# Strassen-Winograd in three more block pairs of one product, with the sum of two branches made by accumulating transfers

## The reference

```python
proj = h @ w_in                 # u, v, q, k, v, gate columns
gate_a, gate_b = jnp.split(jax.nn.sigmoid(gates), 2, axis=-1)
merged = gate_a * (a_out @ w_pa) + gate_b * (b_out @ w_pb)
x = x + merged @ w_o
```

## Time and profile before

| | |
|---|---|
| runs | 1659.09 us median, 1658.59 to 1660.1 |
| profiled execution | 1657.78 us, span 1656.0 us, mean granted clock 0.994 |
| TensorE busy | 1624.0 us (98%) |
| VectorE busy | 1125.3 us (68%) |
| ScalarE busy | 696.1 us (42%) |
| GpSimd busy | 57.6 us (3%) |
| matmuls | 12958, of them 11088 in 462 block products |

### The profile page before, as it was taken

The page is one execution under the profiler, slowest core; times in us unless marked ns, Lnnn a source line. Parts: engine busy times, 40 slices in busy tenths (PEclk is TensorE's granted clock), DMA queues, the critical chain, the costliest instruction groups (busy, mean ns, idle before and its releaser), DMA issues.

```text
span 1656.0 us, 32499 instructions
## 1 busy us (share of the span) xinstructions
PE 1624.0 (98%) x12958; PEld 1584.1 (96%) x12958; DVE 1125.3 (68%) x2053; ACT 696.1 (42%) x1282; POOL 57.6 (3%) x125
## 2 busy tenths in 40 slices
PE   6999999999999999999999999999999999999998
PEld 6999999999999999999999999999999999999997
DVE  6566565656657869652525888888888776767566
ACT  6344444444444426442434544433333334343312
POOL 2000000000000000000012100000000000000001
PEclk8999999999999999999999999999999999999999
DMA  7444434343437774574443233333333327363122
GB/s 246 152 149 117 133 108 135 100 138 101 128 109 206 235 227 154 198 235 132 139 145 107 59 106 105 106 106 106 106 106 104 128 73 267 119 240 104 68 79 109
DMA packets 272473, 227.03 MB, mean 137 GB/s; under 512 B 43336, under 2 KB 223364, under 8 KB 272324
## 3 DMA queue, kind: packets, MB, share of 16 engines
q1 hardware_dynamic: 141054, 158.81, 28.8%
q10 hardware_dynamic: 131269, 66.15, 14.2%
HBM read 150.56 MB, written 74.36 MB: 136 GB/s over the span
## 4 chain that ended last, share of the span: by engine, by line
PE 75%; DVE 2%; DMA 2%; issue 1%; ACT 1%; DVEq 0%; ACTq 0%; POOL 0%; SPq 0%
PE ps L2294 66%; PE ps L2508 3%; DMA lo_f<-g_spill 1%; PE ps L2545 1%; PE ps L2428 1%; PE ps L2370 1%; DMA raw<-in_w_down_dram 1%; PE ps L2400 1%; PE ps L2418 0%; PE ps L2405 0%; PE ps L2388 0%; PE ps L2527 0%; ACT op_hi L1237 0%; DVE w_lo L1605 0%; DVE op_lo L1644 0%
## 5 line engine op out<-in xcount | busy, mean ns | idle before, releaser
L2294 PE MATMUL ps<-op_hi,w_hi 128*128 128x272 f32 x3696 | 780.5, 292 | 14.1 <-issue 5.1
L2294 PE MATMUL ps<-op_hi,w_lo 128*128 128x272 f32 x3696 | 765.9, 289 | 0.0
L2294 PE MATMUL ps<-op_lo,w_hi 128*128 128x272 f32 x3696 | 763.6, 288 | 0.0
L2294 PEld LDWEIGHTS ps<-op_hi,w_hi 128*128 128x128 f32 x3696 | 580.2, 189 | 30.9 <-issue 29.0
L2294 PEld LDWEIGHTS ps<-op_lo,w_hi 128*128 128x128 f32 x3696 | 581.9, 189 | 0.0
L2294 PEld LDWEIGHTS ps<-op_hi,w_lo 128*128 128x128 f32 x3696 | 578.7, 189 | 0.0
L1605 DVE TENSOR_TENSOR w_lo<-raw,w_hi 128x512 fp32r<-128x512 f32 x256 | 174.4, 699 | 177.3 <-ACT w_hi L1203 177.2
L1203 ACT ACTIVATE w_hi<-raw 128x512 fp32r<-128x512 f32 x256 | 153.9, 625 | 129.8 <-PE ps L2294 90.3
L1282 ACT ACTIVATE u<-ps 128x544 f32<-128x544 f32 x100 | 62.4, 624 | 226.0 <-PE ps L2294 225.9
L1203 ACT ACTIVATE w_hi<-w_f 128x512 fp32r<-128x512 f32 x150 | 90.0, 625 | 34.4 <-DVE w_f L1625 29.0
L1605 DVE TENSOR_TENSOR w_lo<-w_f,w_hi 128x512 fp32r<-128x512 f32 x150 | 99.0, 685 | 3.3 <-ACT w_hi L1203 2.9
(11 more groups left out here) (190 smaller groups left out, 1492.3 us busy)
## 6 DMA issues: line engine op xcount, KB each, us to landing
in_spill<-quad SPq DMA_DIRECT2D x88, 272.0 KB, 2.2
raw<-in_w_up_dram ACTq DMA_DIRECT2D x44, 512.0 KB, 5.0
raw<-in_w_in_dram ACTq DMA_DIRECT2D x42, 512.0 KB, 5.3
g_spill<-value_out SPq DMA_DIRECT2D x22, 544.0 KB, 2.7
t_spill<-t_buf SPq DMA_DIRECT2D x8, 1088.0 KB, 4.5
lo_f<-g_spill SPq DMA_DIRECT2D x8, 1088.0 KB, 8.1
lo_f<-t_spill SPq DMA_DIRECT2D x8, 1088.0 KB, 10.3
raw<-in_w_down_dram ACTq DMA_DIRECT2D x16, 512.0 KB, 5.2
```

Source lines behind the costliest of these rows:

```text
L2294: last = pe.matmul(out[:, h, 0:HB], (w_hi, w_lo)[a][place][:, j, :], (op_hi, op_lo)[b][at][:, j, HB * h:HB * h + HB], start=fresh and j == ...
```

## The change

Pairs 27, 28 and 29 leave `PLAIN`: they take seven block products each. Generation 2 is thereby `summed`, so its four operand sums and four more operands (2, 3, 4, 5), high and low, are made. The quadrants of these pairs come from `combine` on VectorE and no longer from `quadrant_out` on ScalarE; `m1c`, `u2` and `u3` are taken for copies, so that no buffers are left for the other branch. The gate buffers become a ring of four, the loads of `load_mb` and the VectorE additions of `merge` go, and a `merge` on GpSimd's queue issues one transfer for each quadrant that reads `mb_spill` and adds to the gated quadrant in SBUF. Each of the 16 transfers waits for its gate and for the transfer before it. Gates 2 and 3 (of pair 26) move to (27, 1, 2), behind the operand low part of block sum 4. The parts of generation 3's operands are made at new places: first "b" part of operand 0 at (29, 4, 2), "b" of operand 1 at (30, 0, 1), "b" of operand 7 at (30, 1, 0), operand 6 at (30, 2, 0). The loading of `w_pa`'s operands isn't changed.

```diff
-PLAIN = (0, 1, PB) + tuple(range(PA, UP)) + (UP,) + tuple(DOWN + 4 * c for c in range(NCHUNK))
+PLAIN = (0, 1, PB, PA) + tuple(range(OUT, UP)) + (UP,) + tuple(DOWN + 4 * c for c in range(NCHUNK))
...
-        gate_buf = (quad[Q11], quad[Q22], m1c)
-        mb_buf = (quad[Q21], quad[Q12], u2)
+        gate_buf = (quad[Q11], quad[Q22], quad[Q21], quad[Q12])
...
                 p, q = numbered(PA, i)
-                dst = (Q11, Q22, None)[i % 3]
-                if i < 2:
+                if i < 4:
+                    dst = (Q11, Q22, Q21, Q12)[i]
                     sp.wait_ge(s_q_out[dst], 16 * store_count(dst, PA))
-                if i == 2 and not plain(PA - 1):
-                    sp.wait_ge(s_comb, 4 * PA)
-                if i >= 3:
-                    sp.wait_ge(s_gated, i - 2)
-                sp.dma_start(gate_buf[i % 3][:], place(in_spill, GA_PAIR + p - PA, q)).then_inc(s_gate_in[i % 3], 16)
-
-            def load_mb(i):
-                p, q = numbered(PA, i)
-                dst = (Q21, Q12, None)[i % 3]
-                if i < 2:
-                    sp.wait_ge(s_q_out[dst], 16 * store_count(dst, PA))
-                if i == 2 and not plain(PA - 1):
-                    sp.wait_ge(s_comb, 4 * PA)
-                if i >= 3:
-                    sp.wait_ge(s_merged, i - 2)
-                sp.wait_ge(s_q_out[q], 16 * store_count(q, p - 3))
-                sp.dma_start(mb_buf[i % 3][:], place(mb_spill, p - PA, q)).then_inc(s_mb_in[i % 3], 16)
+                else:
+                    sp.wait_ge(s_gated, i - 3)
+                sp.dma_start(gate_buf[i % 4][:], place(in_spill, GA_PAIR + p - PA, q)).then_inc(s_gate_in[i % 4], 16)
...
+                    sp.wait_ge(s_gated, 12 + gate_buf.index(quad[q]) + 1)
...
                 if p == PA and (n, j) == (0, 0):
-                    load_mb(0)
                     load_gate_a(1)
-                    load_mb(1)
                     load_gate_a(2)
-                    load_mb(2)
                 if PA <= p <= OUT and (n, j) in ((4, 0), (6, 2), (0, 2), (1, 0)):
 
-                    i = 4 * (p - PA) + {(4, 0): 3, (6, 2): 4, (0, 2): 1, (1, 0): 2}[n, j]
-                    if 3 <= i < 16:
+                    i = 4 * (p - PA) + {(4, 0): 4, (6, 2): 5, (0, 2): 2, (1, 0): 3}[n, j]
+                    if 3 <= i < 16 and i not in (6, 7):
                         load_gate_a(i)
-                        load_mb(i)
+                if p == PA + 1 and (n, j) in ((2, 0), (2, 2)):
+                    load_gate_a(6 + j // 2)
...
+            def merge(i):
+
+                p, q = numbered(PA, i)
+                pool.wait_ge(s_gated, i + 1)
+                pool.wait_ge(s_q_out[q], 16 * store_count(q, p - 3))
+                if i:
+                    pool.wait_ge(s_merged, 16 * i)
+                pool.dma_start(r_q[q][:, p - PA, :], place(mb_spill, p - PA, q), accum_op=ALU.add).then_inc(s_merged, 16)
...
+                if stage(p) == "pa" and (n, j) in ((3, 2), (6, 1), (6, 3)) and (p, n, j) != (PA, 6, 3):
+                    merge(4 * (p - PA) + {(3, 2): 0, (6, 1): 1, (6, 3): 2}[n, j])
+                if PA + 1 < p <= OUT and (n, j) == (0, 2):
+                    merge(4 * (p - 1 - PA) + 3)
+                if p == PA + 1 and (n, j) in ((2, 0), (2, 1)):
+                    merge(2 + j)
...
-                        act.wait_ge(s_merged, raw_ready(g, q, part))
+                        act.wait_ge(s_merged, 16 * raw_ready(g, q, part))
...
-                gate = gate_buf[i % 3]
+                act.wait_ge(s_gate_in[i % 4], 16 * (4 + i // 4 + 1))
+                gate = gate_buf[i % 4]
...
                     square = (m1c, u2)[first_of_half.index(i)]
-                    act.wait_ge(s_gated, 16)
-                    act.wait_ge(s_merged, 16)
...
+                        elif g == 3:
+                            todo = {(1, 2): ((0, "a"),), (2, 2): ((1, "a"),), (4, 2): ((0, "b"),), (5, 0): ((7, "a"),)}.get((n, j), ())
...
+                        elif g == 3:
+                            todo = {(0, 1): ((1, "b"),), (1, 0): ((7, "b"),), (2, 0): ((6, "a"), (6, "b"))}.get((n, j), ())
...
-                            dve.wait_ge(s_merged if g == 3 else s_x1g, raw_ready(g, q, part))
+                            dve.wait_ge(s_merged if g == 3 else s_x1g, (16 if g == 3 else 1) * raw_ready(g, q, part))
...
@@ -1939,15 +1937,7 @@
                 dst = r_q[q][:, p - PA, :]
                 if p == PA and q == Q12 and summed(2):
                     dve.wait_ge(s_op, op_count(2, 4))
-                dve.tensor_tensor(dst, destination(p, q), gate_buf[i % 3][:], ALU.mult).then_inc(s_gated, 1)
-
-            def merge(i):
-
-                p, q = i // 4, numbered(PA, i)[1]
-                dve.wait_ge(s_gated, i + 1)
-                dve.wait_ge(s_mb_in[i % 3], 16 * (i // 3 + 1))
-                dst = r_q[q][:, p, :]
-                dve.tensor_tensor(dst, dst, mb_buf[i % 3][:], ALU.add).then_inc(s_merged, 1)
+                dve.tensor_tensor(dst, destination(p, q), gate_buf[i % 4][:], ALU.mult).then_inc(s_gated, 1)
...
+                        elif g == 3:
+                            lows = {(1, 3): ((0, "a"),), (2, 3): ((1, "a"),), (4, 3): ((0, "b"),), (6, 1): ((7, "a"),)}
...
+                        elif g == 3:
+                            lows = {(0, 2): ((1, "b"),), (1, 1): ((7, "b"),), (2, 1): ((6, "a"), (6, "b"))}
...
-                if stage(p) == "pa" and (n, j) in ((3, 2), (6, 1), (6, 3)):
-                    merge(4 * (p - PA) + {(3, 2): 0, (6, 1): 1, (6, 3): 2}[n, j])
-                if PA < p <= OUT and (n, j) == (0, 2):
-                    merge(4 * (p - 1 - PA) + 3)
...
-                    if stage(p - 1) == "pa":
+                    if stage(p - 1) == "pa" and p - 1 > PA:
                         gate_a(4 * (p - 1 - PA) + 3)
...
-                if kind == "pa" and (n, j) in ((3, 0), (5, 2), (6, 2)):
+                if kind == "pa" and (n, j) in ((3, 0), (5, 2), (6, 2)) and (p, n) != (PA, 6):
                     gate_a(4 * (p - PA) + {3: 0, 5: 1, 6: 2}[n])
...
+                        if (p, n, j) == (PA + 1, 1, 2):
+
+                            gate_a(2)
+                            gate_a(3)
```

More of the change, by code:

```diff
@@ L512, in program @@
         s_mb = sem("s_mb")
-        s_mb_in = sems("s_mb_in", 3)
         s_gated = sem("s_gated")
@@ L724, in load_gate_a @@
                 p, q = numbered(PA, i)
-                dst = (Q11, Q22, None)[i % 3]
-                if i < 2:
+                if i < 4:
+                    dst = (Q11, Q22, Q21, Q12)[i]
                     sp.wait_ge(s_q_out[dst], 16 * store_count(dst, PA))
-                if i == 2 and not plain(PA - 1):
-                    sp.wait_ge(s_comb, 4 * PA)
-                if i >= 3:
-                    sp.wait_ge(s_gated, i - 2)
-                sp.dma_start(gate_buf[i % 3][:], place(in_spill, GA_PAIR + p - PA, q)).then_inc(s_gate_in[i % 3], 16)
-            def load_mb(i):
-                p, q = numbered(PA, i)
-                dst = (Q21, Q12, None)[i % 3]
-                if i < 2:
-                    sp.wait_ge(s_q_out[dst], 16 * store_count(dst, PA))
-                if i == 2 and not plain(PA - 1):
-                    sp.wait_ge(s_comb, 4 * PA)
-                if i >= 3:
-                    sp.wait_ge(s_merged, i - 2)
-                sp.wait_ge(s_q_out[q], 16 * store_count(q, p - 3))
-                sp.dma_start(mb_buf[i % 3][:], place(mb_spill, p - PA, q)).then_inc(s_mb_in[i % 3], 16)
+                else:
+                    sp.wait_ge(s_gated, i - 3)
+                sp.dma_start(gate_buf[i % 4][:], place(in_spill, GA_PAIR + p - PA, q)).then_inc(s_gate_in[i % 4], 16)
             def load_residual(p, q):
                 if p == OUT:
-                    i = max(i for i in range(16) if (quad[q] in (gate_buf[i % 3], mb_buf[i % 3])))
-                    sp.wait_ge(s_gated if quad[q] in gate_buf else s_merged, i + 1)
+                    sp.wait_ge(s_gated, 12 + gate_buf.index(quad[q]) + 1)
                 elif q != Q12:
@@ L1387, in sigmoid_a @@
             def sigmoid_a(i):
-                act.wait_ge(s_gate_in[i % 3], 16 * (4 + i // 3 + 1))
-                gate = gate_buf[i % 3]
+                act.wait_ge(s_gate_in[i % 4], 16 * (4 + i // 4 + 1))
+                gate = gate_buf[i % 4]
                 act.activation(gate[:], gate[:], ACT.Sigmoid).then_inc(s_sig, 1)
@@ L1677, in t_sum @@
                     else:
-                        dve.wait_ge(s_merged if g == 3 else s_x1g, raw_ready(g, Q22, part))
+                        dve.wait_ge(s_merged if g == 3 else s_x1g, (16 if g == 3 else 1) * raw_ready(g, Q22, part))
                     dve.tensor_tensor(lo_f[2][:, j], r22[:, j], lo_f[3][:, j], ALU.subtract).then_inc(s_t, 1)
```

## The result

The changed kernel takes 1670.03 us (median of 4 runs, 1668.5 to 1670.64) against 1659.43 us for the kernel before in the same comparison: a ratio of 1.0068, 95% interval 1.0056 to 1.008. It is 10.6 us slower where 4.6 us less was forecast, and 1 us beyond the range. The profiled execution took 1669.52 us (span 1667.7), 11.7 us more than that of before.

What follows compares the result with a forecast made beforehand. TensorE's instruction stream was taken as the bound, busy 98% of the span. Three products less, 9.0 us, minus stalls of 2.1 (A) and 2.3 (B), none at C: 4.6 us less, 1659.09 to 1654.5 us; range 1650 to 1669.

Steps and rivals of the forecast that it cites:

- What bounds the kernel: Whole span: TensorE's instruction stream, busy 98% of it; the work of the other engines hides behind it.
- the price of a product: On TensorE: 3.007 us each, so three products removed give 9.0 us, all of it on the path.
- Place A: First operand sum at (25, 4, 3): VectorE waits for r12, so product 6 of pair 25 stalls 2.1 us at 714.0.
- SP's wait: SP issues r12 only at 707.44, behind its wait for the weights of pair 26; it lands 5.5 us later.
- Place B: Weight 0 of pair 27: ready late at 745.4, the Q12 read-out at 745.2, wanted at 743.2; a stall of 2.3 us.
- Place C: The chain of transfers on GpSimd, from 755.7 on, toward pairs 29 and 30: a close call, forecast without a stall.
- L: Time of each transfer in GpSimd's chain: taken as 3.6 to 3.9 us, with bounds of 2.7 and 6.7 us.
- the threshold of 3.9: Time per transfer in us up to which nothing is late; beyond it each 0.1 us costs 1.1 us at (29, 4, 2).
- the rival: GpSimd's chain of transfers eats the gain from 4.3 us each: 1662.5 us at 4.5, 1667.5 at 5.0; chance 0.35.
- The worst case of the text: VectorE's long instructions hold up GpSimd while it makes a transfer: 6 us each, over 20 us lost; a small chance.
- The rule of the Trainium skill: A transfer issued on GpSimd takes about 2.0 us plus bytes over 436 GB/s, estimated 2.6 us for 272 KB.
- Rival 3, the clock: TensorE's clock falls behind the two forecast stalls: 1658 us if both are followed by it, no difference; chance 0.14.

Runs made afterwards that it cites:

- the early r12: The changed kernel with r12 for generation 2 loaded ahead of SP's wait for the weights of pair 26: 1670.26 us (4 runs), ratio 1.0069.
- half size: The changed kernel with each of the sixteen transfers adding only the first half of its columns, 136 KB instead of 272 KB: 1659.01 us (one execution).
- the repeat with four semaphores: The changed kernel with each transfer waiting only for the fourth before it, measured again: 1659.38 us (11 runs) against 1658.46, ratio 1.0002.

## Why the prediction was wrong

*What bounds the kernel, and the price of a product*: right. The matmuls fell by 72, and where no wait stands pairs of seven take 21 us.

*Place A*: right in place and releaser (`quad` L1748 at 714; the first sum at 712.08, forecast 713.0), 1.5 us for 2.1. In ten traces with pairs of seven it ranges from 1.1 to 3.2, and follows how late the first sum comes, 9.8 to 11.9 us behind one and the same combination; the two with the early r12 are the two lowest, 1.1 and 1.4. The reason in the text, SP's wait, is a small part of it: without that wait the transfer takes longer instead.

*Place B*: right in place, 1.8 us for 2.3. The third sum came at 734.62 (735.6 forecast), ScalarE's high part of weight 0 at 743.09 (744.1) and the low part at 743.74:

```profile
743.09 0.62 ACT L1199 ACTIVATE w_hi<-raw 128x512 fp32r<-128x512 f32 x1
```

```profile
743.74 0.69 DVE L1603 TENSOR_TENSOR w_lo<-raw,w_hi 128x512 fp32r<-128x512 f32 x1 [2.28 <-ACT w_hi L1199]
```

The difference to the forecast is the 0.6 to 1 us by which A came out shorter.

*Place C*: this is the step that failed, in one term, L = 3.6 to 3.9 us. The text wrote the chain as 10 L + 4.5 us from transfer 2 to transfer 12; it took 53.2 us, so L was 4.87. By the threshold of 3.9 and the two prices given for the rival (8 us at 4.5, 13 at 5.0) that is 11.7 us; the waits at C make 6.7 + 1.6 + 2.5 + 1.1 = 11.9. So the mechanism and its slope were right, its place nearly, and the term that was mis-sized is L: 3.6 to 3.9 us in the text, 4.87 measured. The chain was taken for the unlikelier case. With the addition left out the same arithmetic gives (43.0 - 4.5) / 10 = 3.85, and no wait; at half size 4.14, and a wait of 0.2 us. What L was short of, piece by piece: a plain transfer from GpSimd landed after 3.2 us in this stretch, not 2.7, the value of the earlier trace rows in quiet; the addition cost 1.2 us and not 0.9; and 0.53 us from landing to the next issue was not in the sum at all. Together 4.9, if the medians hold no more of the weight loads than their share. The rows that would have been nearest stood among the transfers of the whole span of before, the loads from SP for the same additions (count, KB, median us to landing):

```profile
quad<-m_spill SPq DMA_DIRECT2D x11, 272.0 KB, 3.5
...
u<-m_spill SPq DMA_DIRECT2D x5, 272.0 KB, 3.3
```

Sixteen loads of the very bytes, with medians of 3.5 and 3.3 us; the earlier trace rows picked two of them, a quick and a slow one, and the text took the quick one. The worst case of the text, links of 6 us by VectorE's long instructions, didn't come: the issue took 0.87 to 1.06 us on GpSimd throughout.

The place that was late first was also not the one named. The text asked for the "b" part of operand 0 at (29, 4, 2); the "a" part of operand 1 at (29, 2, 2) wants transfer 10 and holds up the copy behind it. With nine links to it and 2.3 us from landing to product 4, due at 798.8, its threshold is 755.7 + 9 L + 4.5 + 2.3 = 798.8, L = 4.0, hardly another, and its price at 4.87 is 7.5 us; 6.7 were measured.

*The rule of the Trainium skill* ("DMA: Bandwidth & Descriptors", Anatomy of one DMA), an estimated 2.6 us for a transfer of this size from GpSimd, would have made C free. Here the plain one took 3.2 us and the accumulating one 4.4 by median, and half the bytes of the accumulating one saved 1.0 us, where the rule's bandwidth gives an estimated 0.3.

*Rival 3, the clock*: counted at nothing, since A and B were near the shorter of two waits. Behind A and B it did stay at 1.00 in the trace after the change, but C's waits of 6.7 and 2.5 us brought 1.8 and 1.3 us with them. A wait of 1.8 us at A was followed by 0.94 over 30 us in the kernel without the addition, one of 1.9 us by 0.66 over 5 us in that without the last two additions: waits of that length can go either way. So can longer ones: in the repeat with four semaphores one of 3.2 us at A left the clock at 1.00. The rival should have been tied to the first, not stood by itself. 1654.5 + 11.9 + 3.1 = 1669.5 is the measured time within 0.6 us, partly by luck: A and B came out 1.1 us shorter than this sum has them, and what follows isn't in it.

*Not in the text*: the wait for the power at 951, 1.4 us, and the clock ahead of it, 1.7 us more by the same arithmetic. The lag grew by 2.7 us there in this trace; some executions with the same transfers don't have it.

The chances were the other fault: 35% on the chain, with a bound for L up to 6.7 us, while the low value started from one quiet row of 2.7 us.

## What to carry to other kernels

A chain of transfers that each wait for the last one's landing has a link of landing plus handover plus issue; compare it with the pace of the consumer before looking at anything else, and take the landing from transfers of the same bytes in the same stretch. If the order among them isn't needed, use several semaphores in turn: here that was worth 9 us. And replacing an engine's instruction by a transfer moves its latency onto whoever is next: 0.7 us on VectorE became 4.5 us at the border to pair 30.

## What the runs showed of the hardware that I had not expected

- An accumulating transfer of 272 KB from DRAM to SBUF issued on GpSimd: 0.88 us of issue and 4.4 us to landing by median, against 0.55 and 3.2 for a plain one; half the bytes in the same number of packets, 144: 0.88 and 3.4. The plain one has 80 packets.
- A load of 1088 KB issued 6 us earlier into a stretch at 400 GB/s landed at the same moment, 11.7 us after its issue instead of 5.5, and some 0.4 us sooner by the pace of the stage.
- A run of 18 one-column matmuls (2.0 us) is followed by 3 to 4 us at about half the clock in some executions and not in others, and the first power on GpSimd behind it took 2.0 us in those without, and 2.8 to 13.5 us in those with it.
